# A two-block model on one core: the delta branch's k and q projected first, six weight pieces issued ahead of the barrier

## The reference

```
qkv, z, a, bt = split(u @ w_in)                 # q, k, v, z: 512 columns each; a, bt: 8 each
qkv = silu(depthwise_conv(qkv, conv_w))         # 5 taps along the tokens
q, k, v = split into 4 heads of 128
q = l2norm(q) * 128 ** -0.5;  k = l2norm(k)     # x * rsqrt(sum(x * x) + 1e-6), per head
g = -exp(a_log) * softplus(a + dt_bias);  beta = sigmoid(bt)
o = chunked delta rule(q, k, v, g, beta)        # needs cumulated g, k turned to token rows, v * beta
o = rmsnorm(o) * silu(z)
```

## Time and profile before

| | us |
|---|---|
| median of three runs | 3071.97 (3064.26 to 3077.67) |
| profiled execution | 3062.2 |
| its span, first to last instruction | 3060.4 |
| PE busy | 2581.9 |
| DVE busy | 890.3 |
| ACT busy | 410.5 |

### The profile page before, as it was taken

The page is one execution under the profiler, slowest core; times in us unless marked ns, Lnnn a source line. Parts: engine busy times, 40 slices in busy tenths (PEclk is TensorE's granted clock), DMA queues, the critical chain, the costliest instruction groups (busy, mean ns, idle before and its releaser), DMA issues. The chain is left out here.

```text
span 3060.4 us, 43957 instructions
## 1 busy us (share of the span) xinstructions
PE 2581.9 (84%) x19787; PEld 1396.4 (46%) x19787; DVE 890.3 (29%) x1794; ACT 410.5 (13%) x808; POOL 85.3 (3%) x93
## 2 busy tenths in 40 slices
PE   7969559899999998989899989867568689879995
PEld 4525225334333442434334443335457688555553
DVE  1227533212212222131303130024555542142222
ACT  1031001100101011021201121012013221000001
POOL 0010000000000000000000000000000110000000
PEclk9988678899999999999999999978789799979998
DMA  5316136898998889988998989954001004169997
GB/s 176 119 41 241 63 128 247 343 390 354 391 376 360 349 361 392 356 329 346 386 367 331 369 323 396 363 217 134 1 1 35 2 3 169 60 245 418 422 422 286
DMA packets 158869, 789.19 MB, mean 258 GB/s; under 512 B 18241, under 2 KB 20553, under 8 KB 110937
## 3 DMA queue, kind: packets, MB, share of 16 engines
q1 hardware_dynamic: 155225, 773.78, 63.8%
q0 software_dynamic: 3456, 12.58, 1.0%
HBM read 774.79 MB, written 11.53 MB: 257 GB/s over the span
## 5 line engine op out<-in xcount | busy, mean ns | idle before, releaser
L2947 PE MATMUL bank<-ring,arena 128*34 128x512 f32 (+1 forms) x3072 | 700.0, 598 | 77.3 <-DMA ring<-in_w_up 63.2
L2947 PEld LDWEIGHTS bank<-ring,arena 128*34 128x34 f32 x3072 | 178.5, 117 | 490.0 <-issue 463.9
L2971 PE MATMUL bank<-ring,arena 128*34 128x512 f32 x1408 | 320.6, 597 | 47.2 <-DMA ring<-in_w_down 46.4
L2971 PEld LDWEIGHTS bank<-ring,arena 128*34 128x34 f32 x1408 | 79.0, 112 | 279.0 <-issue 152.0
L303 PE MATMUL bank<-arena,ring 128*128 128x256 f32 (+1 forms) x688 | 160.2, 396 | 11.7 <-DMA ring<-in_w_in 9.6
L303 PEld LDWEIGHTS bank<-arena,ring 128*128 128x128 f32 x688 | 134.9, 197 | 37.2 <-issue 10.4
L3413 PE MATMUL bank<-ring,arena 128*64 128x256 f32 x992 | 111.3, 379 | 4.4 <-DMA ring<-in_moe_w_up 3.6
L2847 PEld LDWEIGHTS bank<-arena 64*64 64x64 f32 x2304 | 76.3, 140 | 53.1 <-issue 52.6
L313 PE MATMUL bank<-ring,arena 128*128 128x512 f32 (+1 forms) x224 | 98.8, 596 | 0.0
L3413 PEld LDWEIGHTS bank<-ring,arena 128*64 128x64 f32 x992 | 73.3, 137 | 46.1 <-issue 14.1
L2959 PEld LDWEIGHTS bank<-consts,arena 34*128 34x128 f32 x704 | 82.7, 191 | 14.9 <-issue 14.1
(11 more groups left out here) (628 smaller groups left out, 3000.5 us busy)
## 6 DMA issues: line engine op xcount, KB each, us to landing
ring<-in_w_gate SPq DMA_DIRECT2D x128, 1408.0 KB, 9.3
ring<-in_w_up SPq DMA_DIRECT2D x128, 1408.0 KB, 12.4
ring<-in_w_down SPq DMA_DIRECT2D x176, 1024.0 KB, 8.5
ring<-in_w_in SPq DMA_DIRECT2D x46, 1024.0 KB, 7.4
ring<-in_moe_w_down SPq DMA_DIRECT2D x33, 1024.0 KB, 15.7
ring<-in_moe_w_gate SPq DMA_DIRECT2D x31, 1024.0 KB, 14.2
ring<-in_moe_w_up SPq DMA_DIRECT2D x31, 1024.0 KB, 16.9
ring<-in_ada_w SPq DMA_DIRECT2D x24, 1024.0 KB, 7.1
```

The costliest lines, as they stand in the source:

```text
L2947: last = mm(ps[c][row:row + CAP, 0:n], xsT[:, e, k, :], w[:, at:at + n], start=k == 0, stop=k == KT - 1)
L2971: last = mm(ps[6][row:row + CAP, :], hidT[:, 2 * j + f, :], w[:, f, half * BANK:(half + 1) * BANK], start=j + f == 0, stop=j == FT // 2 - ...
```

## The change

SP issues the first six of the branch's eight weight pieces right behind the constants' table, ahead of its wait for the barrier; the small tables and the last two pieces stay behind it. The order of the pieces becomes k, q, v, z. PE computes k (banks 0 to 3), q (4 to 7), the gates (bank 2), the two sums of squares of k (banks 0 and 1), v (4 to 7), the two sums of q (0 and 1), z (6 and 7), the transposes of k, the cumulated gates (bank 3) and the transposes of v. DVE normalizes k between the convolutions of q and v, and q after that of v. Squares and roots have two buffers each of their own. ACT takes the roots of k before the silu of q, those of q before the gates, and the silu of v and z after the gates. `settled(ins)` stands for an instruction and the engine's wait for it. The removed lines of the three engines' lists are those of the listing above and are left out here.

```diff
@@ -569,7 +569,7 @@
...
-        sq2 = ar(TOKS2)
+        sq2, roots = ([ar(TOKS2) for _ in range(2)] for _ in range(2))
...
@@ -581,7 +581,7 @@
...
-        gdn_pieces = [column_pieces(A["w_in_2"], g * 512, 512) for g in (1, 2, 0, 3)]
+        gdn_pieces = [column_pieces(A["w_in_2"], g * 512, 512) for g in (1, 0, 2, 3)]
...
@@ -593,7 +593,6 @@
...
-        rhs_flat = gdn_in[0].rearrange("p c t -> p (c t)")[:, 0:TOKS2]
...
@@ -834,12 +833,13 @@
...
+            issue(n_gdn - 8, n_gdn - 2)
...
-            issue(n_gdn - 8, n_gdn)
+            issue(n_gdn - 2, n_gdn)
...
@@ -1215,28 +1215,35 @@
...
+            def columns_act(n):
...
+                for ct in range(4):
+                    last = ACTV(gdn_in[n % 2][:, ct, 2:2 + SEQ], ps[4 * min(n, 1) + ct][:, 0:SEQ], ACT.Copy)
...
+            def silu_of(dst):
+                act.wait_ge(silu_asked, due(act, silu_asked))
+                ACTV(dst, dst, ACT.Silu).then_inc(silu_ready, up(silu_ready))
+            def roots_act():
+                for m in range(2):
+                    act.wait_ge(normed_sum, due(act, normed_sum))
+                    ACTV(roots[m], ps[m][:, :], ACT.Sqrt, bias=eps_col).then_inc(root_ready, up(root_ready))
+            columns_act(0)
+            silu_of(kT)
+            columns_act(1)
+            roots_act()
+            silu_of(qT)
+            act.wait_ge(gdn_in_ready, due(act, gdn_in_ready))
+            columns_act(2)
+            roots_act()
...
+            ACTV(beta, ab[:, :, 8:16], ACT.Sigmoid)
...
@@ -1244,14 +1251,14 @@
...
+            silu_of(vT)
+            act.wait_ge(piece_used, after(gdn_pieces[3]))
+            for t in range(2):
+                last = ACTV(zg[:, t, :], ps[6 + t][:, :], ACT.Silu)
+            last.then_inc(group_read, up(group_read))
...
@@ -1988,60 +1995,67 @@
...
+            def settled(ins):
+                ins.then_inc(dve_order, up(dve_order))
+                dve.wait_ge(dve_order, own(dve, dve_order))
+            def convolved_dve(n):
...
+                    dst = (kT, qT, vT)[n][:, ct, :]
+                    w = lambda j: pc("gdn_conv_2", 12 * j + (4, 0, 8)[n] + ct)
+                    settled(TS(dst, src[:, 0:SEQ], w(0), None, ALU.mult))
...
+                        settled(STT(dst, src[:, j:j + SEQ], w(j), dst, ALU.mult, ALU.add))
...
+            pair_of = lambda x, m: x[:, 2 * m:2 * m + 2, :].rearrange("p h t -> p (h t)")
+            def squares_dve(x):
+                dve.wait_ge(silu_ready, due(dve, silu_ready))
+                for m in range(2):
+                    TT(sq2[m], pair_of(x, m), pair_of(x, m), ALU.mult).then_inc(squared, up(squared))
+            def normed_dve(x, scale):
+                for m in range(2):
+                    dve.wait_ge(root_ready, due(dve, root_ready))
+                    settled(nc.vector.reciprocal(roots[m], roots[m]))
+                    settled(STT(pair_of(x, m), roots[m], scale, pair_of(x, m), ALU.mult, ALU.mult))
+            convolved_dve(0)
+            squares_dve(kT)
+            convolved_dve(1)
+            normed_dve(kT, 1.0)
+            dve.drain().then_inc(turned_read, up(turned_read))
+            squares_dve(qT)
...
+            settled(nc.vector.tensor_copy(ab, ps[2][:, 0:32].rearrange("p (c e) -> p c e", c=2)))
...
+            convolved_dve(2)
...
+            settled(STT(gcol, ab[:, :, 0:8], 0.0, tmp32, ALU.max, ALU.add))
...
+            normed_dve(qT, float(P) ** -0.5)
...
+                settled(nc.vector.tensor_copy(k_tm[:, c], ps[c][:, :].rearrange("p (h e) -> p h e", h=4)))
+            dve.wait_ge(gates_ready, due(dve, gates_ready))
+            nc.vector.tensor_copy(gcum, ps[3][:, 0:16].rearrange("p (c e) -> p c e", c=2)).then_inc(act_asked, up(act_asked))
...
+                    settled(TT(vb[:, d, c], ps[4 + c][:, :].rearrange("p (h e) -> p h e", h=4),
+                               beta[:, c, 4 * d:4 * d + 4].unsqueeze(2).to_broadcast([P, 4, P]), ALU.mult))
+            dve.wait_ge(act_ready, due(dve, act_ready))
+            settled(TT(egb, egb, beta, ALU.mult))
...
@@ -2139,11 +2153,6 @@
...
@@ -3029,43 +3038,47 @@
...
+            def sums_pe():
+                for m in range(2):
+                    pe.wait_ge(squared, due(pe, squared))
+                    mm(ps[m][:, :], C["ones"], sq2[m], start=True, stop=True).then_inc(normed_sum, up(normed_sum))
+            by_feature(pe, 0, gdn_pieces[0], u2x_lat, SEQ)
+            by_feature(pe, 4, gdn_pieces[1], u2x_lat, SEQ)
...
+                    last = mm(ps[2][:, c * 16:(c + 1) * 16], u2x_lat[:, k, c * P:(c + 1) * P], wab[:, k, :], start=k == 0, stop=k == KT - 1)
...
+            sums_pe()
...
+            by_feature(pe, 4, gdn_pieces[2], u2x_lat, SEQ)
+            pe.wait_ge(root_ready, due(pe, root_ready, 2))
+            sums_pe()
+            pe.wait_ge(group_read, due(pe, group_read))
+            by_token(pe, 6, gdn_pieces[3], u2x_lat, TILES2)
+            pe.wait_ge(turned_read, due(pe, turned_read))
+            pe.wait_ge(root_ready, due(pe, root_ready, 2))
+            def turned_pe(src, base):
+                for c in range(2):
+                    for h in range(4):
+                        last = nc.tensor.transpose(ps[base + c][:, h * P:(h + 1) * P], src[:, h, c * P:(c + 1) * P], ident)
+                    last.then_inc(turned, up(turned))
+            turned_pe(kT, 0)
...
+                    last = mm(ps[3][:, c * 8 + 4 * d:c * 8 + 4 * d + 4], C["tri_le" if d == 0 else "tri_ge"],
...
+            pe.wait_ge(silu_ready, due(pe, silu_ready, 3))
+            turned_pe(vT, 4)
+            pe.wait_ge(group_read, due(pe, group_read))
...
```

More of the change, by code:

```diff
@@ L1217, in _ @@
             act.wait_ge(pad_ready2, due(act, pad_ready2))
-            for n in range(4):
+            def columns_act(n):
                 act.wait_ge(piece_used, after(gdn_pieces[n]))
[L1220 to L1228, removed]
-                last.then_inc(group_read, up(group_read))
[L1230 to L1236, removed]
+                for ct in range(4):
+                    last = ACTV(gdn_in[n % 2][:, ct, 2:2 + SEQ], ps[4 * min(n, 1) + ct][:, 0:SEQ], ACT.Copy)
+                last.then_inc(group_read, up(group_read))
+            def silu_of(dst):
[13 more added lines that the diff above has]
+            roots_act()
             act.wait_ge(act_asked, due(act, act_asked))
-            ACTV(beta, ab[:, :, 8:16], ACT.Sigmoid).then_inc(act_order, up(act_order))
-            act.wait_ge(act_order, own(act, act_order))
+            ACTV(beta, ab[:, :, 8:16], ACT.Sigmoid)
             ACTV(tmp32, ab[:, :, 0:8], ACT.Abs).then_inc(act_order, up(act_order))
@@ L1250, in _ @@
             act.wait_ge(act_ready, own(act, act_ready))
[L1251 to L1254, removed]
             act.drain().then_inc(phase_ended, 1)
@@ L1990, in _ @@
                 dve.wait_ge(signal, own(dve, signal))
-            for n in range(3):
-                col = (4, 8, 0)[n]
+            def settled(ins):
+                ins.then_inc(dve_order, up(dve_order))
+                dve.wait_ge(dve_order, own(dve, dve_order))
+            def convolved_dve(n):
                 dve.wait_ge(group_read, due(dve, group_read))
@@ L2023, in _ @@
[L2023 to L2033, removed]
@@ L3043, in _ @@
                 for k in range(KT):
-                    last = mm(ps[0][:, c * 16:(c + 1) * 16], u2x_lat[:, k, c * P:(c + 1) * P], wab[:, k, :], start=k == 0, stop=k == KT - 1)
+                    last = mm(ps[2][:, c * 16:(c + 1) * 16], u2x_lat[:, k, c * P:(c + 1) * P], wab[:, k, :], start=k == 0, stop=k == KT - 1)
             last.then_inc(gates_ready, up(gates_ready))
+            sums_pe()
             pe.wait_ge(group_read, due(pe, group_read))
+            by_feature(pe, 4, gdn_pieces[2], u2x_lat, SEQ)
[11 more added lines that the diff above has]
+            turned_pe(kT, 0)
             pe.wait_ge(cums_ready, due(pe, cums_ready))
@@ L3050, in _ @@
                 for d in range(2):
-                    last = mm(ps[1][:, c * 8 + 4 * d:c * 8 + 4 * d + 4], C["tri_le" if d == 0 else "tri_ge"],
+                    last = mm(ps[3][:, c * 8 + 4 * d:c * 8 + 4 * d + 4], C["tri_le" if d == 0 else "tri_ge"],
                               gcol[:, c, 4 * d:4 * d + 4], start=True, stop=True)
             last.then_inc(gates_ready, up(gates_ready))
-            for n in range(4):
-                pe.wait_ge(squared, due(pe, squared))
-                last = mm(ps[2 + n % 2][:, :], C["ones"], sq2, start=True, stop=True)
-                last.then_inc(normed_sum, up(normed_sum))
-            pe.wait_ge(turned_read, due(pe, turned_read))
-            for m, src in enumerate((kT, vT)):
-                for c in range(2):
-                    if m == 1:
-                        pe.wait_ge(turned_read, due(pe, turned_read))
-                    b = 4 * m + c
-                    for h in range(4):
-                        last = nc.tensor.transpose(ps[b][:, h * P:(h + 1) * P], src[:, h, c * P:(c + 1) * P], ident)
```

(4 more changed lines are left out.)

27 lines of the change are left out of this document (removed).

## The result

| | before | after |
|---|---|---|
| median, us | 3068.11 (four runs, 3062.0 to 3077.67) | 3024.85 (four runs, 3023.02 to 3028.11) |
| profiled execution, its span | 3062.2, 3060.4 | 3026.62, 3024.8 |
| ratio to before, 95% interval | | 0.9857 (0.9827 to 0.9888) |

The kernel became 43.3 us faster by the medians; the sum had said 42.6, and 3029 as the time. The median of the kernel before was 3071.97 for the forecast and is 3068.11 with a fourth run, so 3.9 of the 4.2 us between 3029 and 3024.85 come from the base. The two profiled spans differ by less, 35.6 us, and the stages tell why. In this table "branch" runs from DVE's first memset behind the barrier to the scan's first matmul, "scan" from there to the issue of the next stage's first table, and the other bounds are SP's issues behind barriers.

A forecast was written before the change was run, and what follows sets the result against it. PE bounds the whole; the branch stage half waits for PE, half is a relay between engines. 7.6 us (earlier start) plus 35.0 (order) make 42.6, taken from the median 3071.97: 3029 us forecast, range 3014 to 3042.

The forecast's parts named there:

- the sum: Delta branch's preparation between two barriers: 42.6 us less, 7.6 from the earlier start and 35.0 from the new order.
- The head start: Branch's opening: six weight pieces issued ahead of the barrier let PE start projections at 2051.7, 7.6 us earlier.
- a slow start: PE's first projections: restart at half clock, as in the kernel before, where it costs about 2.1 us.
- The lower end: PE's first projections: a clock already full at the start would be worth 2.1 us more.
- The order: Whole branch stage: the same work rearranged, with DVE carrying the stage, gains 35.0 us.
- the switch of table ahead of k's silu: Ahead of k's squares: DVE waits 2.6 us for k's silu, including 1.28 for ACT's table switch.
- The one gap of 2.6 us: Ahead of k's squares: DVE's only gap, otherwise nearly without idle from 2069 to 2126.
- The covers: Branch stage: PE's and ACT's work stays hidden behind DVE's, PE by 2.0 and 0.8 us, ACT by at least 1.4.
- The thinnest: End of the branch: v's first half turned at 2122.4, wanted by DVE at 2123.2, a cover of 0.8 us.
- the rival in which PE takes over at the end: Branch's end: clock falls ahead of q's sums and PE takes DVE's place; 3031 to 3043 us, chance 0.11.
- The sign that no later stage gives time back: Stages behind the branch: every later stage keeps its length; the forecast is wrong if one gives time back.
- a next stage that opens warmer: Scan's opening, where PE ran slowly for its first 3 us: a possible further gain of at most 1.6 us.

The follow-up runs named there:

- the two kernels with one part: The kernel before with only six weight pieces issued ahead of the barrier: 3058.45 us; the changed kernel with all eight issued behind it: 3030.44 us.

## Why the prediction was right

The forecast's steps stand against the profile of the changed kernel, each in us from DVE's first memset (2051.64 in the forecast, 2055.91 in the profile).

| step | forecast | measured |
|---|---|---|
| PE's first projection | 0.1 | -0.1 |
| convolution of k | 17.7 | 17.1 |
| squares of k | 30.1 | 28.2 |
| convolution of q | 31.5 | 30.8 |
| norms of k | 41.4 | 40.8 |
| convolution of v | 51.5 | 50.6 |
| norms of q | 61.8 | 60.9 |
| products of v | 71.6 | 70.7 |
| scan's first matmul | 75.0 | 73.9 |

**The head start** was right in mechanism and size: 7.6 forecast, 8.2 in the old order, 8.8 in the new. The first includes 0.4 and the second 1.0 us of granted clock, and the kernel before varies by 0.9 in itself. The part that the forecast had left between 0 and 2.1, the granted clock, is visible. Windows of after around PE's restart (columns as in the earlier trace rows):

```profile
2050.00:2053.00 3.00, 2.64 (x13) 2.67 (x14) 1.98 (x5) 0.00 (x0) 0.00 (x0) 0.50 1.04 401
2053.00:2055.00 2.00, 0.70 (x5) 0.46 (x3) 1.89 (x4) 0.00 (x0) 0.00 (x0) 0.94 1.06 395
2055.00:2057.00 2.00, 1.16 (x5) 1.00 (x6) 0.96 (x6) 0.00 (x0) 0.00 (x0) 0.91 1.05 385
2057.00:2059.00 2.00, 2.00 (x6) 1.62 (x5) 0.00 (x0) 0.00 (x0) 0.00 (x0) 0.50 1.05 387
2059.00:2063.00 4.00, 4.00 (x17) 3.41 (x16) 0.00 (x0) 0.00 (x0) 0.00 (x0) 0.87 1.05 384
```

The restart found the clock high (0.91 from 2055 to 2057), it fell to half all the same and was back within 2059 to 2063; two groups took 29.58 us where 27.8 is full speed, a loss of 1.8. The choice of a slow start was right in size, though not in its form: it came a microsecond after the start. The lower end that I had kept is real too: the kernel without reciprocals found the clock high, kept it, and lost 0.1 instead of 1.8. Which of the two a run meets is luck as far as these runs tell: in the other five executions with the new order and the head start the two groups took 29.58 or 29.60. The rise again follows sixteen transposes with PE idle before them (0.50 over 2050 to 2053, while 13 of them run, then 0.94). The Trainium skill says in "TensorE: Matmul & The Clock Gate", Part 4: PE-mode transpose, that transposes do not bring the full clock. The traces agree with it in four of the ten executions (the repeat of the kernel before, the two kernels with one part, and the one with doubled squares), where the clock was still at 0.50 behind the transposes, and disagree in the other six, where it rose in their last microsecond or just behind them. The forecast's sentence that the rise follows them was read from one trace; they can bring the clock and do not always.

**The order** was right: 35.0 forecast and 35.0 measured alone (35.9 by the other execution of the kernel before). That the numbers meet this closely is luck in part. Inside it two terms were off and nearly cancelled. I took the switch of table ahead of k's silu on DVE's path, 1.3 us too much; it had moved ahead of the wait, which the removed line of ACT's list allows and which I had not read out of it. But I also had the copy of q's group ready 0.4 us before DVE asked. DVE asked earlier than forecast, and the copy came 1.26 after the squares instead; so of the 1.3 only 0.2 showed. The one gap of 2.6 us that I had named as a sign became two of 1.26. The convolutions, norms and copies are the same instructions and agree to 0.5 us over the 43 from q's convolution to the end.

**The covers.** Apart from that copy, all that I called hidden was. The thinnest, 0.8 us for the turned v, was computed with transposes at today's slow clock (2.0, 1.8 and 2.0 us); behind the dense projections they ran at full clock, 1.04, 0.95 and 1.07. That step was mis-sized by 2.7 us on the safe side, and with it the chance of 0.11 for the rival in which PE takes over at the end: the added transposes show that it is not near. Where PE is near is earlier, in front of the convolutions of q and v, as the kernel without reciprocals shows.

**Table switches.** ACT has nine in this stage now, each 1.28 us. The Trainium skill's 2.7 us (in "ScalarE: Activation LUTs", Rules for kernel authors) would have made the gain 37.5; it is 43.8, and the trace does not agree with that figure.

**The three small tables**, queued behind six pieces, landed 9.4 to 10.0 us after their issue, 10 to 11 us behind the barrier where the forecast had 11, and PE asked for them at 2085.25, 29 us behind it.

**The base.** I subtracted from the median and not from the profiled execution. That was right, and the profile alone would have misled: its span is only 35.6 shorter, since all that comes ahead of the final norm took 4.28 us longer in that execution, the scan 3.91 and the recurrent branch 1.35. Differences of this kind occur between executions of one kernel as well: the two of the kernel before are 5.78, 2.91 and 1.33 us apart in these three. The sign that no later stage gives time back held but for about 1 us at the scan's opening: I had reckoned only with a next stage that opens warmer, by at most 1.6 us, and it opened colder. The 1.6 is what the kernel with added transposes shows, 7.41 us for the opening against 9.06.

## What to carry to other kernels

When a stage is a relay between engines, lay its work out on the engine with the most of it, and look for what can run beside dense matmuls: here 35 us came from doing the same instructions while PE projected, and DVE's busy time changed by only 0.6 us. Transfers whose buffers are free belong ahead of a barrier that they do not need; what they gave here added to the rest within the spread. Before making the carrying engine lighter, ask how near the next one is: 13.2 us less on DVE gave 4.4, since PE stood right behind it.

## What the runs showed of the hardware

- A switch of ACT's table stood ahead of a wait or behind it, depending on the instructions around it: with the engine's wait for its own copies in front of the wait for DVE it came behind (2.57 us from convolution to silu's end before, a gap of 2.60 with the wait put back), without it ahead (1.26 us).
- This stage of short bursts of matmuls has its own spread: the scan took 127.6 to 133.0 us in ten executions with the same instructions on PE, and length less PE's busy time was 48.64 or 48.65 us in the three shown.
- The same matmuls cost what the clock at their place makes them cost: eight transposes took 1.04 us behind the projections (granted clock 1.00), and half of 3.94 us after the old order's gaps (0.50); the scan's first 64 matmuls took 7.41 to 10.14 us.
- PE kept working from 2055.84 on and was still given half clock from 2057 to 2059 (0.50 in the row above). In the kernel without reciprocals it started in the same way, after 1.83 us idle instead of 2.14, and kept the full clock.
- A reciprocal of 128x512 floats takes DVE 3.35 us, a product 0.69.
